# Cross-attention to route 0 by token halves: two bank pairs in the output projection, head 1 in raw fp32, value slots between the last query pieces

## The reference, cut to what matters

```
x  = rms_norm(h, norm_x_g)
q  = (x @ w_xq)                      # 4 heads of 128
p  = softmax(q k^T / sqrt(128))      # keys and values from mem @ w_xkv
h  = h + (p v) @ w_xo
xn = rms_norm(h, norm_ffn_g)
q  = xn @ peer_wq                    # 8 heads of 256
s1, s2 = q[..., :128] @ keys1.T, q[..., 128:] @ keys2.T
v1, i1 = top_k(s1, 16); v2, i2 = top_k(s2, 16)
sc, ci = top_k(v1[..., :, None] + v2[..., None, :], 16)   # of 256 sums
e  = i1[ci // 16] * 128 + i2[ci % 16]                     # 16 of 16384 experts
a  = gelu(U[e] . xn)
h  = h + sum over heads and experts of softmax(sc) * a * V[e]
```

## Time and profile before

| | |
|---|---|
| median of 3 runs | 2268.74 us (2264.98 to 2269.31) |
| profiled execution | 2264.38 us |
| its span | 2262.6 us, granted TensorE clock 0.992 of full speed |
| busy: TensorE, VectorE, ScalarE, GpSimd | 1894.2, 1326.3, 608.1, 733.9 us |
| moved by DMA | 700.81 MB, of it 537.32 MB by GpSimd's queue |
| read from HBM | 698.11 MB |

### The profile page before, as it was taken

One profiled execution on the slowest core, in us unless ns is written; L12 is line 12 of the kernel. 1 busy time (PEld: TensorE's weight loads), 2 busy tenths in 40 slices (PEclk: granted clock), 3 DMA queues, 4 the chain that ended last, 5 costly groups with the idle time before them and its releaser, 6 DMA issues.

```text
span 2262.6 us, 22868 instructions
## 1 busy us (share of the span) xinstructions
PE 1894.2 (84%) x6683; PEld 1125.3 (50%) x6683; DVE 1326.3 (59%) x2182; ACT 608.1 (27%) x1068; POOL 733.9 (32%) x629
## 2 busy tenths in 40 slices
PE   7999999999999998997777777777777777777777
PEld 6888787777778786643232222222222222222222
DVE  5544556777766556674655654664665566466444
ACT  4544445555544344211111111111111111111101
POOL 1000000110000001344545545555554564556542
PEclk9999999999999999999999999999999999999999
DMA  8566743444345763799999999999999999999998
GB/s 268 174 187 196 221 144 97 116 117 120 111 147 170 240 197 100 267 414 371 415 422 411 419 422 411 417 416 423 419 422 422 421 422 422 421 422 422 421 421 340
DMA packets 160381, 700.81 MB, mean 310 GB/s; under 512 B 15520, under 2 KB 19648, under 8 KB 94032
## 3 DMA queue, kind: packets, MB, share of 16 engines
q0 software_dynamic: 74144, 537.32, 57.4%
q1 hardware_dynamic: 85616, 161.89, 23.0%
q10 hardware_dynamic: 576, 1.05, 0.1%
HBM read 698.11 MB, written 2.10 MB: 309 GB/s over the span
## 4 chain that ended last, share of the span: by engine, by line
PE 42%; DMA 36%; issue 10%; DVE 8%; ACT 2%; POOL 1%; SPq 1%; DVEq 0%; POOLq 0%; ACTq 0%
DMA v_ring<-in_peer_v_dram,idx_v 19%; DMA big<-in_peer_u_dram,idx_u 14%; PE banks L665 9%; PE banks L667 9%; PE banks L666 9%; PE banks L1064 6%; PE banks L1034 3%; PE banks L783 2%; DMA wq<-in_peer_wq_dram 1%; PE banks L645 1%; DMA wraw<-in_w_xkv_dram 1%; PE banks L774 1%; PE banks L767 1%; DVE product L1913 1%; POOL v_ring L562 1%
## 5 line engine op out<-in xcount | busy, mean ns | idle before, releaser
L1064 PE MATMUL banks<-v_ring,kxT 128*128 128x512 f32 x1920 | 888.7, 606 | 304.1 <-DMA v_ring<-in_peer_v_dram,idx_v 303.1
L1913 DVE SCALAR_TENSOR_TENSOR product<-big,xn 128x2048 f32<-128x2048 f32 x256 | 586.9, 2293 | 418.6 <-DMA big<-in_peer_u_dram,idx_u 413.1
L1064 PEld LDWEIGHTS banks<-v_ring,kxT 128*128 128x128 f32 x1920 | 346.6, 190 | 845.6 <-ACT kxT L1425 388.2
L553 POOL DMA_INDIRECT big<-in_peer_u_dram,idx_u x256 | 363.0, 1418 | 287.4 <-PE banks L1064 126.3
L1507 DVE TENSOR_TENSOR ws<-wraw,ws 128x1024 fp32r<-128x1024 f32 (+1 forms) x264 | 317.1, 1205 | 226.5 <-ACT ws L1113 224.1
L562 POOL DMA_INDIRECT v_ring<-in_peer_v_dram,idx_v x240 | 288.4, 1202 | 339.7 <-PE banks L1064 288.9
L1425 ACT ACTIVATE kxT<-ident,ga 128x128 f32<-128x128 f32 x240 | 96.4, 403 | 1029.8 <-PE banks L1064 1026.8
L1113 ACT ACTIVATE ws<-wraw 128x1024 fp32r<-128x1024 f32 (+1 forms) x264 | 272.3, 1035 | 270.9 <-PE banks L667 223.2
L665 PE MATMUL banks<-ws,xr 128*128 128x512 f32 x768 | 308.2, 401 | 6.8 <-DVE ws L1507 2.3
L667 PE MATMUL banks<-ws,xr 128*128 128x512 f32 x768 | 300.3, 391 | 0.0
L666 PE MATMUL banks<-ws,xr 128*128 128x512 f32 x768 | 300.0, 391 | 0.0
(11 more groups left out here) (268 smaller groups left out, 1488.6 us busy)
## 6 DMA issues: line engine op xcount, KB each, us to landing
wraw<-in_w_in_dram SPq DMA_DIRECT2D x152, 512.0 KB, 3.6
wraw<-in_w_out_dram SPq DMA_DIRECT2D x32, 512.0 KB, 4.0
wq<-in_peer_wq_dram SPq DMA_DIRECT2D x24, 512.0 KB, 10.7
wraw<-in_w_xkv_dram SPq DMA_DIRECT2D x16, 512.0 KB, 7.5
wraw<-in_w_branch_da_dram SPq DMA_DIRECT2D x16, 512.0 KB, 3.7
wraw<-in_w_branch_nsa_dram SPq DMA_DIRECT2D x16, 512.0 KB, 4.0
wraw<-in_w_xq_dram SPq DMA_DIRECT2D x8, 512.0 KB, 3.6
wraw<-in_w_xo_dram SPq DMA_DIRECT2D x8, 512.0 KB, 3.7
```

The costliest lines, as they stand in the source:

```text
L553: nc.gpsimd.indirect_dma_start(u_ring[:, r, :], None, peer_u[0], bass.IndirectOffsetOnAxis(ap=idx_u[par][:, j:j + 1], axis=0)).then_inc(u_ ...
L1064: last = nc.tensor.matmul(V_BANKS[c][n], diag[:, r, :], v_ring[:, r, n * NW:(n + 1) * NW], start=(first and j == 0), stop=(final and j == ...
L1913: V.scalar_tensor_tensor(out=product, in0=u_ring[:, r, :], scalar=1.0, in1=xn3[:, par, :], op0=ALU.mult, op1=ALU.mult, accum_out=dots[:, p ...
```

## The change

What it does, in the order of the program:

- Query product (`xq_piece`): pieces 0 to 3 for both halves, 4 to 7 for half 0, then 4 to 7 for half 1 with half 0's attention between them. ScalarE and VectorE have the matching order; the last three splits of the tile and the first of the next stand between steps of the attention.
- Output projection (`xo_pass`, `xo_out`): a pass is one tile for one half; even tiles use B[0] and B[1], odd ones B[4] and B[5]. Adds, gains, transposes and splits go by half.
- Head 0 (`h0_piece`): all of half 0, then half 1; queries, transposes, scores by half. Route 0 needs half 0's scores alone.
- Head 1 (`h1_piece`): raw fp32, from `xf`. Its four pieces and those of tiles 1 to 3 (28, `RAWS`) use 11 slots: the eight of `wq` and three in free memory.
- GpSimd computes the norms' square roots between the adds of the last quarter. The value gathers wait for `xf` and for head 0's four pieces.
- Route 1 moves behind product 5 of unit 0; softmax weights and `weigh` move too.
- Value slots 0 to 2 of unit 0 stand behind raw pieces 5, 6, 7 of tile 3 on TensorE, slot 3 behind the transposes, the rest behind the scores.

The diff, cut to its core:

```diff
+def raw_slot(g):
+    if g < HP:
+        return g
+    return 8 + g - HP if g < HP + 3 else (g - 3) % 8
@@ sync: raw pieces
+            sp.wait_ge(ev_done, 48 + X_H + 1)
+            for g in range(HP, HP + 2):
+                raw_piece(g)
+            for b in range(2):
+                sp.wait_ge(tp_ready[b], (G_OX + b) // 2 + 1)
+            raw_piece(HP + 2)
+            for g in range(HP):
+                sp.wait_ge(w_split, T_PQ * PIECES + g + 1 + WR)
+                raw_piece(g)
+            for g in range(HP + 3, 2 * HP + 3):
+                sp.wait_ge(w_used, T_PQ * PIECES + (g - HP - 3) // 2 + 1 + WR)
+                raw_piece(g)
+            for g in range(2 * HP + 3, RAWS):
+                sp.wait_ge(wq_used, g - 10 if g < 15 else g - 7)
+                raw_piece(g)
@@ gpsimd
-            pool.wait_ge(w_used, (T_PQ + 1) * PIECES + WR)
+            pool.wait_ge(w_used, T_PQ * PIECES + HP + WR)
+            pool.wait_ge(xf_done, 8)
             both_rows(1, 1)
@@ tensor
+            xq_piece(WR, 1)
+            xq_piece(WR + 1, 1)
+            qx_transposes(0)
+            xq_piece(WR + 2, 1)
...
+            XS(0), XS(1)
+            xq_piece(WR + 3, 1)
+            qx_transposes(1)
+            XT(0)
...
+            XS(2), XS(3), XT(1), XV(0), XV(1)
+            ox_transposes(0)
+            XT(2), XT(3), XV(2)
...
+            xo_pass(0, 0)
+            XV(3)
+            ox_transposes(1)
+            evacuated(G_OX + 1)
+            xo_pass(0, 1)
+            for n in range(1, X_H):
+                x3_transposes(n - 1, 0)
+                xo_pass(n, 0)
+                x3_transposes(n - 1, 1)
+                xo_pass(n, 1)
+            x3_transposes(3, 0)
+            h0_piece(0, 0), h0_piece(1, 0)
+            x3_transposes(3, 1)
+            h0_piece(2, 0), h0_piece(3, 0), h0_piece(0, 1)
+            h0_transposes(0)
+            h0_piece(1, 1)
+            h0_scores(0)
+            h0_piece(2, 1), h0_piece(3, 1), h1_piece(0)
+            h0_transposes(1)
+            h1_piece(1)
+            h0_scores(1)
+            h1_piece(2), h1_piece(3), raw_tile_piece(1, 0)
+            h1_transposes()
+            raw_tile_piece(1, 1)
+            h1_scores()
+            for i in range(1, N_PQ):
+                for n in range(2 if i == 1 else 0, PIECES):
+                    raw_tile_piece(i, n)
+                    if i == N_PQ - 1 and n >= PIECES - 3:
+                        v_slot(0, 0, n - PIECES + 3, first=True)
+                for c in range(C):
+                    tile_transposes(i, c)
+                if i == N_PQ - 1:
+                    v_slot(0, 0, 3)
+                tile_scores(i)
+            v_step(0, 0, skip=RING)
@@ scalar
+            x_query(0)
+            hi(5, T_XQ)
+            x_query_T(0)
+            hi(6, T_XQ)
+            x_exps(0), x_exps(1)
+            x_query(1)
+            hi(7, T_XQ)
+            copy_pt(48, 0, 4, 1)
+            x_query_T(1)
+            copy_pt(49, 1, 4, 1)
+            x_exps(2), x_exps(3)
+            copy_pt(50, 2, 4, 1)
+            ox_hi(0)
+            copy_pt(51, 3, 4, 1)
+            hi(0, T_XO)
+            ox_hi(1)
...
+            h0_query(0)
+            h0_evac(0)
+            h0_query(1)
+            h0_evac(1)
             route_softmax(0)
...
             route_softmax(1)
             with act.Fori(1, N_PQ - 1) as i:
                 query_tile(i)
...
             gelu(0, 0)
+            act.wait_ge(ga_ready, 1)
+            diagonals(0, 0, range(0, RING))
             query_tile(N_PQ - 1)
@@ vector
+            def xo_out(n, c):
...
+                V.tensor_tensor(h[:, c, cols], B[4 * (n % 2) + c], h[:, c, cols], ALU.add).then_inc(acc_free[c], 1)
+                dve.wait_ge(acc_free[c], T_XO + n + 2)
+                dve.sem_inc(h_done, 1)
+                V.tensor_tensor(xn3[:, c, cols], h[:, c, cols], grow[:, cols], ALU.mult).then_inc(xn_done, 1)
...
+            lo(5, T_XQ)
+            XMX(0), XMX(1)
+            lo(6, T_XQ), lo(7, T_XQ)
+            XMX(2), XMX(3), XEV(0), XEV(1)
+            ox_lo(0)
+            XEV(2)
+            XEV(3)
+            dve.wait_ge(grow_landed, 16)
+            lo(0, T_XO)
+            ox_lo(1)
+            xo_out(0, 0)
+            lo(1, T_XO)
+            xo_out(0, 1)
+            for n in range(1, X_H):
+                lo(2 * n, T_XO)
+                x3_lo(n - 1, 0)
+                xo_out(n, 0)
+                x3_lo(n - 1, 1)
+                lo(2 * n + 1, T_XO)
+                xo_out(n, 1)
+            lo(0, T_PQ)
             for c in range(C):
...
+                x3_lo(3, c)
+                mean_squares_h(3, (c,))
...
             for j in range(PK):
                 dot(0, 0, j)
+                if j == 1:
+                    route_weights(0, 0)
+                if j == 5:
+                    dve.wait_ge(tp_free[1], (G_PQ + 3) // 2 + 2)
+                    route(1, scores[:, 256:512], 1)
+                if j == 10:
+                    route_weights(1, 1)
```

More of the change, by code:

```diff
@@ new lines, in h0_transposes, with h0_scores @@
+            def h0_transposes(c):
+                pe.wait_ge(act_steps, 8 + c)
+                transposes(G_PQ + 2 * c, [(stage_b[:, c, t * P:(t + 1) * P], t * P) for t in range(2)])
+            def h0_scores(c):
+                evacuated(G_PQ + 2 * c)
+                bank = tp_begin(G_PQ + 2 * c + 1)
+                for half in range(2):
+                    last = nc.tensor.matmul(bank[:, half * P:(half + 1) * P], qpT[:, half, c * P:(c + 1) * P], keysT[:, half, :],
+                                            start=True, stop=True)
+                last.then_inc(tp_ready[1], 1)
@@ L1413, in _ @@
+            for c in range(C):
+                act.wait_ge(acc_free[c], A_PQ + 2)
+            act.sem_inc(act_steps, 1)
+            evac(G_PQ + 4, qpT[:, 2:4, :], B[2].rearrange("p (t s) -> p t s", t=2))
+            evac(G_PQ + 5, scores[:, 2 * HW:4 * HW], B[3])
             route_softmax(1)
```

425 lines of the change are left out of this document (222 added, 203 removed).

## The result

| | before | after |
|---|---|---|
| median | 2267.65 us (2264.98 to 2269.31, 5 runs) | 2253.97 us (2253.16 to 2254.20, 5 runs) |
| profiled execution, its span | 2264.38, 2262.6 | 2253.16, 2251.3 |
| first gather issued (G) | 933.50 | 926.10 |
| from G to the end of the span | 1329.1 | 1325.2 |

The ratio is 0.994 with a 95% interval of 0.9926 to 0.9955: faster by 13.7 us, where 11.7 was forecast. The median lies 1.3 us above the forecast 2252.7.

A forecast was written before the change was run, and what follows sets the result against it. The end was taken as set by the first gather's time (G), the bytes left after it and DMA idle time after it. -11.9 (G) + 2.7 (DMA loss) - 2.5 (bytes) = -11.7, from 2264.4 to 2252.7 us; range 2244 to 2262.

The forecast's parts named there:

- Attention by halves: Cross-attention: first projection matmul 1.5 us earlier (868.5 against 870.05), half 1's pass until 878.1; alone worth next to nothing.
- Projection: Output projection on two bank pairs, by halves: tile period from 8.0 to 6.5 us, last gains 3.5 us earlier.
- my 1.5 us for the adds: Projection: GpSimd's fp32 adds slow VectorE by 1.5 us in total; bounds 0 and 14 us.
- Rival 3: Nothing left: GpSimd's eight adds each hold VectorE 1.76 us, 14 in all; end near 2265, with part 2261 to 2268; chance 0.08.
- Head part: Head 0 by halves, head 1 raw: last gain to copied scores falls from 18.5 to 8.6 us, 9.9 gained.
- G moved: First gather comes 11.9 us earlier (3.5 + 9.9 - 1.5), from 933.5 to about 921.6.
- After G: From first gather on: DMA loss 13 to 14 us, 2.7 more than before; fewer query bytes save 2.5 us.
- Route 1 between the products 2: After the first gather: route 1 standing between unit 0's products costs 2 us of DMA loss.
- Arrival of slot 0 2 to 3 + 2 x 2.1 + 2: DMA loss around the first value slots: 2 to 3 us for slot 0's arrival, plus 2 x 2.1 and 2.
- Rival 1: The hole at 1030 to 1042 closes; only start and routes cost, 5 us instead of 13.5; end 2244; chance 0.20.
- Rival 4: Late query pieces starve the value slots and idle the DMA; at 7.5 us a piece the end is 2274; chance 0.06.
- rival 2: Projection keeps its 8 us; first gather gains about 7, end 2258; a clock dip could cost 1.6 us; chance 0.16.

The follow-up runs named there:

- second set of runs: The changed kernel, unchanged, timed again on the chip of the next two experiments: 2252.57 us (5 runs), ratio to before 0.9935.
- four parts: Changed kernel with route 1 cut into four parts behind products 1, 3, 5 and 7 of unit 0: 2252.75 us, ratio to before 0.9937.

## Why the prediction was right, point by point

**The total was right, partly by luck.** I subtracted 11.7 us from a profiled execution that lay 3.3 us below the median of the kernel before. From the median, 2267.65, the same sum gives 2256.0, 2.0 above what was measured. Behind the landmark the change gained 17.5 us in the two profiles, not 11.7. The medians, which average over the part ahead, differ by 13.7 and, in the second set of runs, by 15.5. That is 2 to 4 us less than behind the landmark. A median cannot be split there, so where these went is not shown.

**Attention by halves: "worth next to nothing" was too kind.** The first projection matmul came 2.8 us earlier than before, where I had 1.5. Of this 1.5 is this part's (33.9 with the attention whole, 32.4 with it by halves), and the other 1.4 (35.2 against 33.9) I put down to half 0's pass, which by the code no longer waits for half 1's output. Yet the whole part costs 2.6. I had seen that half 1 comes later and let it pass, since it would end "about where tile 0 ended before". But tile 0 before ended late for another reason, the granted clock's dip, which let its 24 matmuls take 7.3 us instead of 5.7. Against an undipped tile, half 1's late pass is a loss on the chain.

**Projection: right on the chain, wrong on its cure and its size.** The period went from 8.0 to 7.2, where I had 6.5. That the banks chained the tiles was right. Before, TensorE stood 1.4 us ahead of each tile, until VectorE's add had emptied the bank:

```profile
885.77 0.47 PE L665 MATMUL banks<-ws,oxr 128*128 128x512 f32 x1 [1.39 <-DVE h L1848]
...
893.78 0.47 PE L665 MATMUL banks<-ws,oxr 128*128 128x512 f32 x1 [1.36 <-DVE h L1848]
```

After, no projection matmul from the second tile on waits for an add, and none does with one bank pair either: half 0's add falls under half 1's pass. So what broke the chain is the passes by halves, and the second pair, which I named as the reason, added nothing to them. Without GpSimd's adds beside it, half 1's adds follow each other by 6.4 to 6.7, so my 6.5 and my 1.5 us for the adds (measured 1.7) were sound. In total the last gain came 2.8 us earlier; 5.4 by passes by halves and an undipped clock, minus 2.6 by the attention.

The Trainium skill (SBUF — State Buffer, "two separate sides") has a VectorE operation with two SBUF inputs and a GpSimd operation that reads SBUF exclude each other for whole instructions, the first to start holding the other back. My prediction took the 1.71 us row to speak against that, and this was a misreading: the rows agree with the rule to within 0.15 us. Take the fences of the fourth tile above. GpSimd's add of 901.83 ran its plain 1.30 us, and the gain that began inside it, 0.69 us by itself, ended 0.54 us behind the add's end. The low part of 904.20 kept its 1.21; the add that began inside it, 1.30 by itself, ended 1.16 behind the low part's end; and the gain that began inside that add ended 0.55 behind it. The adds to h, which read one operand from a bank, took 0.68 beside an add of GpSimd as without one. Rival 3 went wrong by the order of events, not by the rule: each of GpSimd's adds started beside an add to h or a low part, so only its last 0.64 us or less fell on a gain. In the three tiles that held five gains back, by 0.48, 0.49, 0.49, 0.27 and 0.27 us, 2.0 us together, where the run with the adds late shows 1.7. Another order of the same operations could have cost far more.

**Head part: right.** 18.5 to 7.6 us, predicted 8.6. Moving half 0's scores back by two pieces cost 3.7, predicted 3.5 to 4.5.

**G moved** 13.6 us against the landmark, predicted 11.9.

**After G: the size was wrong, and its sign.** I put the loss up by 2.7 us and took 2.5 for bytes. Measured: loss 10.8 to 9.3, and one query piece less after G (15 of 28 instead of 16 of 24), 1.2 us; from G to the end 3.9 us less. Two terms of the sum were mis-sized. "Route 1 between the products 2" measured 6.4: four rows in flight last 10 us, route 1 with the product behind it keeps the next slot from coming free for 13.6, and the gather into it took 2.94 us to issue instead of 0.94 (more on this at the end). These make 5.6 of the 6.4, an estimate from the rows. "Arrival of slot 0 2 to 3 + 2 x 2.1 + 2", 8 to 9 us together, measured 0.0: slot 0 was used 94.8 after G, as forecast (95.4), but GpSimd, held back by the early hole, had not run out of slots by then. The runs with route 1 first and with four parts show the link: take the early hole away and 3.6 to 6.3 us of loss appear at the slots. The two errors were of one stock of bytes, counted once too small and once too large. A smaller gain I did not foresee: before, TensorE stood 1.1 and 2.3 us for two late query pieces, at G + 82 and G + 88, and after for none.

Rival 1 (the hole closes) came nearest to what the slots did; its 8 us were not there, since the early hole took 6.4. Rival 4 did not occur: the raw pieces landed in 8.0 us at the median and 27.7 at most, and TensorE never stood for one after G. The clock term of rival 2, a dip in half 1's first pass, came in three of the twelve profiles and cost 1.2 to 1.3 us.

**Ahead of the landmark.** The same work ended at 834.8 and 841.2 in two profiles of the kernel before, at 836.5 and 841.6 in two of one variant, and at 838.8 to 842.2 in ten profiles of the changed kernel and its other variants. The granted clock goes with it. Over 0 to 55, 300 to 352 and 630 to 675 us it was 0.94, 0.93 and 0.96 in the first profile of the kernel before and 0.91, 0.90 and 0.85 in its second. Counted as length x (1 - granted clock) from zero to the landmark, 10.2 us were lost where the landmark stands at 834.8, 13.7 at 836.5, 15.4 at 838.8, and 17.1 to 20.5 in the eleven profiles with 840.7 to 842.2. Since the kernel before shows both ends, the edit is not needed for it. What decides in one execution whether the clock dips, and whether the changed kernel dips more often, is open.

## What to carry to other kernels

Compare two traces from the last point that the change cannot have touched, not from zero; here that turned a difference of 11 us into one of 17. Then hold the result against the medians, which here say 13.7 and 15.5. Where rings bound what can be in flight, a hole in the transfers is a symptom: closing it gains only if what is short over the whole stretch gains too (here, as argued and not shown, TensorE until its last query scores). And when work is split into halves to start earlier, cost the half that ends later, against the case without its accidents.

## What the runs showed of the hardware

- **A gather that GpSimd begins to issue inside one of VectorE's products is not issued before the product has ended.** These two are of the changed kernel, one with VectorE in a product, one while it waited for rows:

```profile
965.07 2.94 POOL L588 DMA_INDIRECT big<-in_peer_u_dram,idx_u  x1 [12.64 <-DVE product L2103]
...
975.94 0.94 POOL L588 DMA_INDIRECT big<-in_peer_u_dram,idx_u  x1 [0.30 <-issue]
```

  The four issues from 965.07 on, 2.10 to 2.94 us long, ended 0.81 or 0.82 us after the end of the product that ran when they began. So did the rest: of the 512 gathers of this execution 211 began inside a product, and every one ended 0.80 to 0.84 us after that product's end, while 221 that overlapped no product took 0.94 us at the median. The products kept 2.29 us throughout. No run took the products away, but the count leaves little room for another cause. Over the whole kernel the key gathers average 1.44 us.
- **GpSimd's fp32 add and VectorE's operation on two SBUF inputs did not run at the same time either.** In the fourth tile whichever began second ended later than the first's end by its own length, less 0.15 us; an operation with one operand in a bank was not held.
- **The granted clock is not a function of the order.** The same TensorE instructions with the same thin stretch ahead saw 0.53 in one execution and 1.00 in another, a difference of 1.3 us on the path.
- **An identical prefix of some 840 us varies by up to 7.4 us** between executions, more than most terms of this change, and most of it goes with how long the granted clock stood at its lower level. Between the landmark and the last gain, 2.9 us was the most by which executions with the same edits there differed, and the granted clock shows where.
